# A two-layer decoder trunk on one core: the up-projection by Strassen block products, the projections around it with tokens on the partitions

## The reference

```python
def trunk_layer(x, ...):
    h = x @ w_in                                  # 1024 -> 1792
    # columns of h: gated chunks of 128 positions, and sliding-window attention with rotary and sinks
    mix = concat([gmlp_out, attn]) @ w_out        # 1024 -> 1024
    x = layer_norm(ALPHA * x + mix, ln1_g, ln1_b)
    up = x @ w_up                                 # 1024 -> 2 * 2816
    hp = concatenate([conv_prefix, up], axis=1)
    hc = conv_b + sum(conv_w[i] * hp[:, i:i + T] for i in range(3))
    g, u = hc[..., :D_FF], hc[..., D_FF:]
    y = (gelu(g) * u) @ w_down                    # 2816 -> 1024
    x = layer_norm(ALPHA * x + y, ln2_g, ln2_b)
```

## Time and profile before

| | us |
|---|---|
| median of three runs | 2580.12 |
| least and most | 2577.29, 2584.52 |
| the profiled execution | 2586.85 |
| its span, first to last instruction | 2585.1 |
| TensorE busy | 2416.6 |
| VectorE busy | 1621.9 |
| ScalarE busy | 753.4 |
| GpSimd busy | 575.3 |

### The profile page before, as it was taken

One profiled execution on the slowest core, in us unless ns is written; L12 is line 12 of the kernel. 1 busy time (PEld: TensorE's weight loads), 2 busy tenths in 40 slices (PEclk: granted clock), 3 DMA queues, 4 the chain that ended last, 5 costly groups with the idle time before them and its releaser, 6 DMA issues.

```text
span 2585.1 us, 39049 instructions
## 1 busy us (share of the span) xinstructions
PE 2416.6 (93%) x14492; PEld 2306.4 (89%) x14492; DVE 1621.9 (63%) x2232; ACT 753.4 (29%) x1306; POOL 575.3 (22%) x252
## 2 busy tenths in 40 slices
PE   7999887899999999999999988879999999999995
PEld 7997687899999999999799758879999999999993
DVE  1579768655665656555636894875566555566566
ACT  2236534312122222212332472432221221212224
POOL 1111144311222221221131103522221121121212
PEclk9999888999999999999999998989999999999997
DMA  6211232111011111110031203301111111001101
GB/s 166 64 48 38 67 97 70 49 50 44 15 48 49 49 49 49 41 49 33 18 79 42 70 18 101 114 25 50 50 49 49 41 49 49 29 28 49 49 25 70
DMA packets 133524, 137.78 MB, mean 53 GB/s; under 512 B 25864, under 2 KB 124008, under 8 KB 133352
## 3 DMA queue, kind: packets, MB, share of 16 engines
q1 hardware_dynamic: 133424, 136.50, 17.9%
HBM read 124.94 MB, written 7.89 MB: 51 GB/s over the span
## 4 chain that ended last, share of the span: by engine, by line
issue 68%; POOL 14%; PE 9%; DVE 6%; DMA 1%; ACT 1%; POOLq 1%; SPq 0%; DVEq 0%; ACTq 0%
POOL wl L503 10%; PE ps L1350 4%; POOL wdl L518 4%; DVE stat L883 1%; PE ps L1373 1%; PE ps L1588 1%; PE ps L1390 1%; DVE stat L877 1%; DVE stat L886 1%; DVE hT L889 1%; DVE hT L880 1%; DVE xl L892 1%; PE ps L1394 1%; DMA xin<-in_x_prompt 0%; PE ps L1365 0%
## 5 line engine op out<-in xcount | busy, mean ns | idle before, releaser
L1350 PE MATMUL ps<-xh,wh 128*128 128x384 f32 (+1 forms) x2656 | 879.1, 331 | 14.7 <-POOL wl L503 13.6
L1350 PE MATMUL ps<-xh,wl 128*128 128x384 f32 (+1 forms) x2656 | 871.1, 328 | 0.0
L1350 PE MATMUL ps<-xl,wh 128*128 128x384 f32 (+1 forms) x2656 | 870.0, 328 | 0.0
L503 POOL TENSOR_TENSOR wl<-wraw,wh 128x1024 fp32r<-128x1024 f32 x166 | 428.3, 2581 | 1137.1 <-ACT wh L576 1137.1
L1350 PEld LDWEIGHTS ps<-xh,wh 128*128 128x128 f32 x2656 | 502.3, 189 | 30.3 <-issue 28.0
L1350 PEld LDWEIGHTS ps<-xl,wh 128*128 128x128 f32 x2656 | 502.3, 189 | 0.6 <-issue 0.4
L1350 PEld LDWEIGHTS ps<-xh,wl 128*128 128x128 f32 x2656 | 501.6, 189 | 0.0
L1212 DVE TENSOR_TENSOR hT<-hT,ps 128x384 f32<-128x384 f32 (+1 forms) x528 | 279.0, 532 | 299.5 <-PE ps L1350 299.2
L1350 PE MATMUL ps<-ah,wdh 128*128 128x384 f32 (+1 forms) x1056 | 347.2, 329 | 6.1 <-DVE al L1272 6.1
L1350 PE MATMUL ps<-ah,wdl 128*128 128x384 f32 (+1 forms) x1056 | 345.4, 327 | 0.0
L1350 PE MATMUL ps<-al,wdh 128*128 128x384 f32 (+1 forms) x1056 | 345.3, 327 | 0.0
(11 more groups left out here) (195 smaller groups left out, 2810.1 us busy)
## 6 DMA issues: line engine op xcount, KB each, us to landing
wraw<-in_w_up SPq DMA_DIRECT2D x44, 1024.0 KB, 8.3
wdraw<-in_w_down SPq DMA_DIRECT2D x44, 512.0 KB, 3.6
...
```

The lines of the kernel that those rows point to most:

```text
L503: pool.tensor_tensor(wl[slot % 2][:], wraw[par_][:, :, 128 * (slot % 2):128 * (slot % 2) + 128], wh[slot % 2][:].bitcast(F32), ALU.subtrac ...
L1350: e = nc.tensor.matmul(out, lhs, rhs, start=(m == 0), stop=(m == n - 1))
```

## The change

Nearly all of the program is written anew; the in-projection, the gated chunks and the attention keep their instructions.

**Out-projection.** The stationary operand is now a tile of activations, 128 features by 128 tokens (`m_tile`), the moving one 512 columns of a row block of w_out. The nine token tiles (the ninth has the 64 sample tokens) run in three groups `G3`; each tile has two PSUM banks for its 1024 output columns. A unit is one of 8 row blocks (512 KB), with 3 tiles x 3 products x 2 halves = 18 matmuls. Two slots hold `rh` and `rl`. The last two units of a group alternate by tile, so that the tiles end one after the other.

**First norm.** Tokens lie on the partitions: VectorE adds ALPHA times x, which SyncE brings from DRAM into `rzc`, to PSUM (`summed`), takes statistics with two BN_STATS and a BN_AGGR; ScalarE takes the root and scales (`normal`). The normalised tile goes to `z_scr` in DRAM, is transposed by TensorE (`turn_z`, 8 transposes a tile), and ScalarE applies gain and offset while it copies it from PSUM, piece by piece (line 760).

**Up-projection.** The token dimension is halved (512 and 512), the features are halved, and w_up is taken as gate and up columns. VectorE forms four sums of activations once per layer (`operand_sums`), GpSimd four sums of weight blocks per pair f of column blocks (`sums`), 22 pairs. Seven products (`big`, 12 matmuls with 512 moving columns each) replace eight, and VectorE joins them in seven steps (`joined`). Each of the eight weight blocks is rounded by ScalarE and its remainder formed by VectorE or GpSimd. The 64 sample tokens are four plain products of their own with 64 moving columns (`small`, 12 matmuls each).

**Convolution.** The first tap runs on ScalarE, two on VectorE, over prompt and samples at once (1104 columns). The gated result goes to `a_scr` in DRAM.

**Down-projection and second norm.** It begins after the whole up-projection, in the form of the out-projection: 3 groups of 22 units, w_down read three times, activations read back from `a_scr`, four slots of weights, three of activations. At the seventh unit of the first group SyncE fetches gains and offsets, broadcast over the partitions, and three tiles of z. The second norm goes with tokens on the partitions too; the result goes to `y_scr` and is turned for layer 1 (`turn_x`), or is sent out.

The diff, cut to its core:

```diff
-        xh = new("xh", [P, KD, T], F32R)
-        wh = [new(f"wh{i}", [P, KD, P], F32R) for i in range(2)]
...
+G3 = [(0, 1, 2), (3, 4, 5), (6, 7, 8)]
+KORD = [4, 5, 6, 7, 0, 1, 2, 3]
...
+        z_scr = nc.dram_tensor("z_scr", [T, D], F32, kind="Internal").ap()
+        y_scr = nc.dram_tensor("y_scr", [T, D], F32, kind="Internal").ap()
+        a_scr = nc.dram_tensor("a_scr", [FT, P, CV], F32, kind="Internal").ap()
...
+                    if d == 6:
+                        sp.wait_ge(S["rows_out"], 96 * (FT // 2) * (l + 1))
+                        for q in range(2):
+                            sp.wait_ge(S[f"a_out{q}"], 16 * (FT // 2) * (l + 1))
+                        for n, v in enumerate((ln1_g, ln1_b, ln2_g, ln2_b)):
+                            sp.dma_start(gain[n][:], v[l].partition_broadcast(P)).then_inc(S["gain_landed"], 16)
+                        for t in G3[0]:
+                            z_back(l, t)
...
+            def sums(l, f):
+                pool.tensor_tensor(a22, a22, a21, ALU.add).then_inc(S["u_sum"], 1)
+                pool.wait_ge(S["u_sum"], n + 1)
+                pool.tensor_tensor(a21, a11, a21, ALU.subtract).then_inc(S["u_sum"], 1)
+                pool.wait_ge(S["u_sum"], n + 2)
+                pool.tensor_tensor(a11, a22, a11, ALU.subtract).then_inc(S["u_sum"], 1)
+                pool.wait_ge(S["u_sum"], n + 3)
+                pool.tensor_tensor(a12, a12, a11, ALU.subtract).then_inc(S["u_sum"], 1)
...
+            def hi_out(l, c):
+                act.wait_ge(S[f"wc_landed{(c + 2) % 4}"], wc_count(l, c))
+                if c < 2:
+                    act.wait_ge(S["in_done"], l * 3 * INT + 39 + 3 * c)
+                else:
+                    name, count = used_c(l, c - 2)
+                    act.wait_ge(S[name], count)
+                act.activation(rh[c % 2][:], wrow[(c + 2) % 4][:], ACT.Copy).then_inc(S["w_hi"], 1)
...
+                act.wait_ge(S["z_tr"], l * NTOK + t + 1)
+                for k in range(KD):
+                    e = act.activation(mix[:, k, rows_of(t)], ps[:, 6 + k // 4, P * (k % 4):P * (k % 4) + tokens(t)],
+                                       ACT.Identity, scale=lnp[:, k:k + 1], bias=lnp[:, 8 + k:9 + k])
+                e.then_inc(S["xf_ev"], 1)
...
+            def summed(l, which, t):
+
+                n, i, q = ln_n(l, which, t), t % 3, tokens(t)
+                rz = (rzd if which else rzc)[i]
+                if which:
+                    dve.wait_ge(S["xp"], l * NTOK + t + 1)
+                    dve.wait_ge(S["d_done"], l * NTOK + t + 1)
+                else:
+                    dve.wait_ge(S[f"rz_landed{i}"], 16 * (6 * l + t // 3 + 1))
+                    dve.wait_ge(S["c_done"], l * NTOK + t + 1)
+                dve.scalar_tensor_tensor(out=rz[0:q, :].rearrange("p (b n) -> p b n", n=512), in0=rz[0:q, :].rearrange("p (b n) -> p b n", n=512),
+                                         scalar=ALPHA, in1=ps[0:q, 2 * i:2 * i + 2, :], op0=ALU.mult, op1=ALU.add).then_inc(S["ln_r"], 1)
+                dve.wait_ge(S["ln_r"], n + 1)
+                for half in range(2):
+                    e = dve.bn_stats(out=bnst[0:q, i, 6 * half:6 * half + 6], in_=rz[0:q, 512 * half:512 * half + 512])
+                e.then_inc(S["ln_bn"], 1)
+                dve.wait_ge(S["ln_bn"], n + 1)
+                dve.bn_aggr(out=mv[0:q, i, :], in_=bnst[0:q, i, :]).then_inc(S["ln_ag"], 1)
+
...
+                t1, t2, t3, t4 = (btf[:, 24 + 4 * i:28 + 4 * i, cols] for i in range(4))
+                dve.wait_ge(S["xf_ev"], l * NTOK + t + 1)
+                dve.tensor_tensor(t1, b12, b11, ALU.subtract).then_inc(S["t_sum"], 1)
+                dve.tensor_tensor(t3, b22, b12, ALU.subtract).then_inc(S["t_sum"], 1)
+                dve.wait_ge(S["t_sum"], n + 1)
+                dve.tensor_tensor(t2, b22, t1, ALU.subtract).then_inc(S["t_sum"], 1)
+                dve.wait_ge(S["t_sum"], n + 3)
+                dve.tensor_tensor(t4, b21, t2, ALU.subtract).then_inc(S["t_sum"], 1)
...
+                if out == "u2":
+                    dve.wait_ge(S["snap_g"], n + 1)
+                    dve.tensor_tensor(g2, g1, bank(M6), ALU.add).then_inc(S["u_u2"], 1)
+                elif out == "c11":
+                    dve.wait_ge(S["u_u2"], n + 1)
+                    dve.tensor_tensor(g1, g1, bank(M2), ALU.add).then_inc(S["u_c11"], 1)
+                elif out == "u3":
+                    dve.wait_ge(S["u_u2"], n + 1)
+                    dve.tensor_tensor(u1, g2, bank(M7), ALU.add).then_inc(S["u_u3"], 1)
+                elif out == "c12a":
+                    dve.wait_ge(S["u_u3"], n + 1)
+                    dve.tensor_tensor(g2, g2, bank(M5), ALU.add).then_inc(S["u_c12a"], 1)
+                elif out == "c22":
+                    dve.wait_ge(S["u_u3"], n + 1)
+                    dve.tensor_tensor(u2, u1, bank(M5), ALU.add).then_inc(S["u_c22"], 1)
+                elif out == "c21":
+                    dve.wait_ge(S["u_c22"], n + 1)
+                    dve.tensor_tensor(u1, u1, bank(M4), ALU.add).then_inc(S["u_c21"], 1)
+                else:
+                    dve.wait_ge(S["u_c12a"], n + 1)
...
+            def six(i, q, left, right, first, final):
+
+                (lh_, ll_), (rh_, rl_) = left, right
+                for m, (lhs, rhs) in enumerate(((lh_, rh_), (lh_, rl_), (ll_, rh_))):
+                    for half in range(2):
+                        e = nc.tensor.matmul(ps[0:q, 2 * i + half, :], lhs, rhs[:, 512 * half:512 * half + 512],
+                                             start=(first and m == 0), stop=(final and m == 2))
+                return e
...
+                    right = [out_unit(KD * g + KD - 2), out_unit(KD * g + KD - 1)]
+                    for i in range(3):
+                        e = out_six(g, i, KD - 2, right[0])
+                        if i == 2:
+                            e.then_inc(S["c_used"], 1)
+                        out_six(g, i, KD - 1, right[1]).then_inc(S["c_done"], 1)
...
-                    gemm(UP0 + 4 * i + sl, (UP0 + sl) % 2, sl % 2, lambda: pe.wait_ge(S["up_ev"], BEFORE + tt - 1))
...
+                def big(b, right, bank):
+                    n = 3 * HK
+                    m = 0
+                    for k in range(HK):
+                        (lh_, ll_), (rh_, rl_) = left(b, k), right[k]
+                        for lhs, rhs in ((lh_, rh_), (lh_, rl_), (ll_, rh_)):
+                            e = nc.tensor.matmul(ps[:, bank, :], lhs, rhs, start=(m == 0), stop=(m == n - 1))
+                            m += 1
+                    e.then_inc(S["u_p"], 1)
+
+                def small(f, b, k0, col, first):
+                    m = 0
+                    for k in range(HK):
+                        (lh_, ll_), (rh_, rl_) = left(b, k), (xs[:, k0 + k, :], xs[:, 8 + k0 + k, :])
+                        for lhs, rhs in ((lh_, rh_), (lh_, rl_), (ll_, rh_)):
+                            e = nc.tensor.matmul(ps[:, 6 + f % 2, col:col + NS], lhs, rhs, start=(first and m == 0),
+                                                 stop=(not first and m == 3 * HK - 1))
+                            m += 1
...
+                    small(f, B_22, HK, NS, True)
+                    ready(f, B_21)
+                    small(f, B_21, 0, NS, False)
+                    if f:
+                        rows_turn(f - 1)
+                        pe.wait_ge(S["u_c22"], n)
+                    ready(f, B_S2)
+                    big(B_S2, t2, up_bank(f, M6))
+                    ready(f, B_S1)
+                    if f:
+                        pe.wait_ge(S["u_u3"], n)
+                    big(B_S1, t1, up_bank(f, M5))
+                    ready(f, B_S3)
+                    if f:
+                        pe.wait_ge(S["u_c12"], n)
+                    big(B_S3, t3, up_bank(f, M7))
+                    ready(f, B_S4)
+                    pe.wait_ge(S["snap_g"], n + 1)
...
+                def down_six(g, i, k, unit):
+                    (h_, l_), right = unit
+                    q = tokens(3 * g + i)
+                    return six(i, q, (h_[:, P * i:P * i + q], l_[:, P * i:P * i + q]), right, k == 0, k == FT - 1)
```

2026 lines of the change are left out of this document (1112 added, 914 removed).

## The result

The changed kernel takes 2635.22 us (median of four runs, 2631.33 to 2641.40) against 2582.32 for the kernel before on the same chips. The ratio is 1.0204, 95% interval 1.0171 to 1.0238, so it is slower by 2.0%. The forecast was 2602 and slower by 0.85%: the sign and the range from 2530 to 2665 held, the size did not.

The account below looks back on a forecast made before the run. TensorE, busy 2416.6 of 2585.1 us, was taken as the bound; stream +19.6, waits +4, clock +28, starts -6 and +4, end -27 gave +23, so 2608 us, scaled to 2602 (0.85% slower), range 2530 to 2665.

Parts of the forecast that it names:

- Part 2 (a): Out-projection: TensorE's waits for rounding and remainder with two weight slots, and half clock behind them; 26 us per layer.
- Part 2 (d): Down-projection: waits at unit 2, behind SyncE's burst with its half clock, and at two group ends; 15 us per layer.
- Part 4: Both ends and layer 1's start: earlier first products -6 us, late tiles in layer 1 +4, shorter end -27.
- Part 3: Up-projection: narrow products cost the clock in 17 of 44 pairs of column blocks; +28 us.
- rival B: Up-projection: narrow products quick, 62 ns each giving 2462 us, or 81 ns giving 2530; 12% with the 81 ns form.
- Rival A: Up-projection: the clock holds through the narrow groups, so not slower; 2574 us, chance 30%.
- layer 1's start: Start of layer 1: its last three tiles normed and turned some 5 us too late; +4 us.
- Part 2 (b): First norm of the last three tiles, exposed behind the out-projection: 19 us idle, 2.5 half clock; 21 us per layer.
- (c): Up-projection steady state: 24.8 us per pair of column blocks, with 5 us of waits per layer.
- Rival D: Up-projection: VectorE becomes the bound at 27 us a pair instead of 24.8; 2699 us, chance 5%.
- Rival C: Up-projection: the clock is lost in nearly every pair; +45 us, 2647 us, chance 8%.
- E: Out- and down-projection: queues wait twice as much as worked; +40 us, 2642 us, chance 10%.

Follow-up runs that it names:

- e9_eight: Changed kernel with the last of the seven block products of each pair computed twice into the same bank; 2759.21 us.
- e3_merge: Changed kernel with high and low parts of the samples side by side behind one weight load, 8 products per group instead of 12; 2559.44 us.
- e10_three: Changed kernel with three groups of the samples' narrow products (36) in one row in each pair from the second on; 2658.57 us.
- e2_group: Changed kernel with all four groups of the samples' narrow products (48) in one row in every pair; 2737.93 us.
- e5_turns: Changed kernel with tiles of x turned between the products of each chunk instead of three in a row ahead of them; 2625.56 us.
- e6_burst: Changed kernel with the four gains and three tiles of z issued one per unit, units 6 to 12, instead of all behind unit 6; 2618.52 us.
- e7_order: Changed kernel with ScalarE rounding layer 1's first two in-projection weight tiles one unit earlier, ahead of the second norm's square roots; 2626.28 us.
- e1_drop: Changed kernel without 11 of every 12 products of the samples' up-projection, so their rows are not computed; 2519.87 us.

## Why the prediction was right or wrong

The size failed at the waits and the start: Parts 2 (a) and (d) and both terms of Part 4 for the starts came out 16.6, 18.3, 21 and 8 us longer than worked, over both layers. The clock term of Part 3 failed the other way, by 25. What each one had wrong follows.

**Right: the prices.** 226.7 and 115 ns against 226.7 and 112 measured. The step that took the narrow product from load durations (the difference between widths as the loading, plus 8) held within 3 ns; with it rival B, quick narrow products at 62 or 81 ns, falls. The Trainium skill (TensorE: Matmul & The Clock Gate, Back-to-back issue gap) has 81 ns for 128 columns and 131 for 512; for these f32r products the trace disagrees, with 112 ns for 64 columns and 227 for 512. The Trainium skill's load of columns / 1.2 ns (same page, LDWEIGHTS), 107 ns for 128, is 5 below the measured distance, and the trace agrees with it to that. That seven products save 60 us and the samples cost more than that is the core of the result, and e9_eight and e3_merge show both halves.

**Wrong: Part 3, the clock.** +28 was taken; measured is one stretch of half clock in each layer, in the first pair, +3. Rival A's mechanism was the true one. The step that failed took the rows of 24 narrow products for like the 44 transposes of before, because both last 2.7 us; the changed kernel loses the clock behind its 44 transposes and not behind its 24 products. The argument against (full clock through the attention's small products) was the better one. e10_three and e2_group show how near the edge was: with 36 and 48 in a row the kernel took 23 and 103 us more.

**Wrong: Part 4, the start.** -6 was taken; measured +15, 21 us more and the largest of the misses that made the kernel longer. I had read from the earlier trace rows that DMA was the limit of the first 29 us, and took the turned groups of three as a plain gain. They are not: each turn needs ScalarE's and VectorE's pass over one pair of banks, 2.46 us of idle time, two times in layer 0's second and third group each, and with each group goes a stretch at half clock, 10.2 us long, which reaches 5 and 6 us into the products. The products do start 9.4 us earlier (19.89 against 29.27), but the two groups then hold TensorE for 10.1 and 8.8 us (31.03 to 41.11 and 51.93 to 60.74), and the step had put both the turns and their waits at nothing. The kernel before did all its turns ahead of the first product, while x was still coming in. e5_turns gives back 8.7 us of the 21; the rest is not taken apart by a run.

**Mis-sized: Part 2 (a), the out-projection.** 26 of waits, measured 34. The two waits that I had worked (3.9 and 2.5) came at 3.72 and 2.27 in the second group; in the third the 3.9 came at 5.10. Missing were four smaller ones behind the turned tiles of z (1.24, 1.80, 1.18, 1.30), also for GpSimd's remainder, and half clock for 23.8 us in all.

**Mis-sized: Part 2 (d), the down-projection.** 15, measured 23 and 25. The burst cost 6.81 and 8.75 of waiting where 6 was worked, with half clock of 6.8 and 10.2 us behind it; e6_burst puts it at 9.0 and 12.6 us in all, where the term had 6 + 3.4. The larger part of the miss is the rest. The wait of unit 2 came at 1.72 for 2.4 and those of the group ends at 1.60 and 1.64 for 1.5, but one for activations at unit 4 (2.19) and one at the last pair of units (3.03) had not been seen; without the burst 14.2 and 12.5 us are left above the products and transposes, where 5.4 was worked.

**Mis-sized: layer 1's start.** +4 for tiles that would come late; measured +12. Not the tiles but the order in ScalarE's queue, which the step did not look at although the code shows it: with the order changed (e7_order) the stretch is 46.6 us, below the 47.3 of the prediction.

**Right: Part 2 (b) and (c) and the end.** 21 at the first norm against 20, 5 in the steady state against 1, 15 us at the end against 14.3. That an exposed norm only changes its place held: 27.9 us from one stretch to the next, TensorE busy for 9.85. The 18 us of idle time there are near the 19 worked, but not at one place: 4.31 us stand ahead of the first block product, for GpSimd's remainder, 3.09 ahead of a turned tile, and at the first M4 only

```profile
486.53 1.19 PE L1869 MATMUL ps<-bt,bh 128*128 128x512 f32 x2 [10.26 <-issue]
```

which the trace puts down to no engine; in the code TensorE waits there for VectorE's remainders of the operands, as the prediction had it.

Rival D (VectorE the bound) did not occur. VectorE works 18.0 us a pair in the changed kernel, 17 was worked; its joins hold TensorE only where a pair would be shorter than about 20.4 us (e1_drop). Rival C did not occur. E's mechanism, queues of the out- and down-projection that wait longer than worked, did: 35 us, and it stood at 10%. Its price was wrong as well: twice the waits of (a) and (d) would be 41 us more in each layer, 82 in all and not 40. C's +45 should be +42 by the prediction's own 1.6 us a pair, and the 2608 scales to 2603; neither matters.

That the forecast came out with the right sign was luck: the clock term, too high by 25 us, stood in for part of the 57 us that were missing. Rival A, which had the clock right, would have been wrong in sign for lack of them.
